# Routing of a mixture-of-experts layer built from unnormed rows, three token blocks ahead of the last

## What is computed

```python
x = x + jnp.concatenate([attn, ssm], axis=-1) @ w_out[i]
x = x + moe_ffn(rms_norm(x, norm_ffn[i]), w_router[i], b_router[i], ...)

def moe_ffn(h, w_router, b_router, w_gate, b_gate, w_up, b_up, w_down, b_down):
    t = h.reshape(-1, d)
    logits = (t @ w_router + b_router).astype(jnp.float32)
    top_val, top_idx = lax.top_k(logits, TOP_K)
    top_w = jax.nn.softmax(top_val, axis=-1)
    ...                      # the tokens of each expert are gathered
    g = jnp.minimum(xb @ w_gate[e] + b_gate[e], SWIGLU_LIMIT)
    u = jnp.clip(xb @ w_up[e] + b_up[e], -SWIGLU_LIMIT, SWIGLU_LIMIT)
    act = g * jax.nn.sigmoid(SWIGLU_ALPHA * g) * (u + 1.0)
    return act @ w_down[e] + b_down[e]   # weighted, scattered back, added
```

## Time and profile before

| | |
|---|---|
| median of 3 runs | 1453.48 us (1450.92 to 1461.56) |
| profiled execution | 1453.4 us, span 1451.6 us |
| mean granted TensorE clock | 0.954 |
| TensorE busy | 1320.3 us (91%) |
| VectorE, ScalarE, GpSimd busy | 443.3, 217.6, 192.5 us |
| moved by DMA | 446.16 MB, mean 307 GB/s |
| chain that ended last | TensorE 71%, SyncE's weight issues 19%, DMA 3% |

### The profile page before, as it was taken

How to read it: one execution, slowest core, us unless ns; L and a number is a source line. 1 busy time by engine, 2 the same in 40 slices (tenths; PEclk the granted TensorE clock), 3 DMA queues, 4 the chain that set the end, 5 groups by cost and what they waited for, 6 DMA issues and landing times.

```text
span 1451.6 us, 40133 instructions
## 1 busy us (share of the span) xinstructions
PE 1320.3 (91%) x18029; PEld 787.9 (54%) x18029; DVE 443.3 (31%) x1030; ACT 217.6 (15%) x491; POOL 192.5 (13%) x148
## 2 busy tenths in 40 slices
PE   5999989996799999899999999999999997876763
PEld 3466676664456656565666666666655554443321
DVE  3653576553322223122132312222222232112110
ACT  2222244341101110101010111111110110100000
POOL 0001300000102211211112121211111211111000
PEclk9999999997799999899999999999999999999765
DMA  8000420019899999999999999999999999999993
GB/s 344 3 1 0 163 88 1 30 49 347 310 352 376 382 391 401 391 393 360 389 387 392 381 381 391 363 385 383 386 386 388 392 380 398 398 395 393 402 406 136
DMA packets 128494, 446.16 MB, mean 307 GB/s; under 512 B 13218, under 2 KB 21474, under 8 KB 128322
## 3 DMA queue, kind: packets, MB, share of 16 engines
q1 hardware_dynamic: 113202, 426.37, 75.5%
q0 software_dynamic: 15120, 17.20, 5.6%
HBM read 433.29 MB, written 14.94 MB: 309 GB/s over the span
## 4 chain that ended last, share of the span: by engine, by line
PE 71%; SPq 19%; DMA 3%; DVE 2%; issue 2%; POOL 1%; ACT 1%; DVEq 0%; POOLq 0%; ACTq 0%
PE pair L1789 46%; SPq L596 18%; PE pair L1548 8%; PE pair L1532 4%; PE pair L1509 2%; PE pair L1640 2%; DMA ring<-in_w_down 1%; PE pair L1749 1%; PE pair L1729 1%; DMA ring<-in_w_in 1%; PE pair L1761 1%; PE pair L1652 1%; DVE rest L1032 1%; POOL ring L699 1%; DMA out<-rest 1%
## 5 line engine op out<-in xcount | busy, mean ns | idle before, releaser
L1789 PE MATMUL pair<-ring,rest 128*32 128x256 f32 x14864 | 864.0, 387 | 52.2 <-DMA ring<-in_w_down 20.1
L1789 PEld LDWEIGHTS pair<-ring,rest 128*32 128x32 f32 x14864 | 473.3, 111 | 391.4 <-issue 46.4
L1032 DVE TENSOR_TENSOR rest<-pair,rest 128x512 f32<-128x512 f32 (+5 forms) x122 | 90.6, 743 | 515.2 <-PE pair L1789 465.5
L751 POOL DMA_INDIRECT out<-rest x82 | 128.5, 1567 | 826.4 <-ACT rest L989 753.6
L1548 PE MATMUL pair<-ring 128*128 128x512 f32 (+1 forms) x320 | 125.3, 550 | 0.0
L989 ACT ACTIVATE rest<-rest 128x256 f32<-128x256 f32 x82 | 36.5, 500 | 568.1 <-DVE rest L1032 568.1
L1548 PEld LDWEIGHTS pair<-ring 128*128 128x128 f32 x320 | 60.3, 190 | 60.4 <-issue 58.8
L1032 DVE TENSOR_TENSOR rest<-rest 128x512 f32<-128x512 f32 (+7 forms) x98 | 62.4, 649 | 34.3 <-ACT rest L971 26.7
L971 ACT ACTIVATE rest<-rest 128x512 f32<-128x512 f32 (+3 forms) x34 | 24.4, 718 | 298.1 <-DVE rest L1341 298.1
L1789 PE MATMUL pair<-rest 128*32 128x256 f32 x880 | 55.7, 395 | 5.7 <-DMA rest<-in_w_gate 3.0
L1532 PE MATMUL pair<-ring 128*128 128x512 f32 x128 | 55.4, 594 | 0.0
(11 more groups left out here) (171 smaller groups left out, 807.0 us busy)
## 6 DMA issues: line engine op xcount, KB each, us to landing
ring<-in_w_up SPq DMA_DIRECT2D x121, 1024.0 KB, 17.3
ring<-in_w_gate SPq DMA_DIRECT2D x120, 1024.0 KB, 15.4
ring<-in_w_down SPq DMA_DIRECT2D x120, 1024.0 KB, 17.9
rest<-in_w_gate SPq DMA_DIRECT2D x8, 1024.0 KB, 17.4
rest<-in_w_down SPq DMA_DIRECT2D x8, 1024.0 KB, 15.9
rest<-in_w_up SPq DMA_DIRECT2D x7, 1024.0 KB, 16.1
ring<-in_w_in SPq DMA_DIRECT2D x1, 4160.0 KB, 15.5
ring<-in_x SPq DMA_DIRECT2D x8, 512.0 KB, 5.9
```

The source lines that it names most:

```text
L751: p.indirect_dma_start(out=out_rows, out_offset=bass.IndirectOffsetOnAxis(ap=sidx[vi.ring][:, g:g + 1].bitcast(I32), axis=0), in_=yrow[:, ...
L1032: return v.tensor_tensor(out=out, in0=a, in1=b, op=op)
L1789: last = T.matmul(ps[q * TOK:(q + 1) * TOK, g * QW:(g + 1) * QW], x, pieces[slot][:, kk, q * QW:(q + 1) * QW], start=(k == 0 and g % 2 == ...
```

## The change

- The router logits no longer wait for the norm. TensorE transposes the sum rows x1 themselves: half `th..a` inside the second half of the output projection (ahead of its last two k-slices), half `th..b` one step later; `th` and `lg` move one step forward. The gain `norm_ffn` is multiplied into the router matrix once by GpSimd (new; one more small DMA at the start brings it), and rstd is applied when the logits are read. `hrw` is still computed and stored as before.
- Choosing the top 4, weights and payload are done per tile on VectorE and ScalarE (`choose`, `weigh`; GpSimd's seven operations go). For tiles 0 to 2 they run while TensorE projects tile 3, with a new prefix product (`cue`, six matmuls) between the two halves of that projection.
- After the last logits only `cum` of tile 3, the last one-hot tile and the dispatch of expert 0 stand ahead of its gather. The order of the experts is computed behind it.
- `replicate` of expert 0, `dispatch` and `replicate` of expert 1 move from ahead of the products into the first gate product (ahead of k-slices 1, 2 and 3), the overflow table into the first up product. `dispatch` of expert j+2 moves from k-slice 4 to 5.
- Weight pieces 13 and 14 are issued after the `normed_rows` stores have landed, with 15 and 16.

```diff
-        for first, name, parts in ((TM, "tm", "ab"), (OP, "op", "ab"), (TH, "th", "ab"), (LG, "lg", " ")):
+        for first, names in ((TM, ("tm{}a", "tm{}b")), (OP, ("op{}a", "op{}b", "th{}a")), (TH, ("th{}b",)), (LG, ("lg{}",))):
...
-TM, OP, TH, LG = 7, 8, 10, 11
+TM, OP, TH, LG = 7, 8, 9, 10
...
             sp.wait_ge(s_ost, 16 * NT)
-            for n in (13, 14):
-                load(n, STREAM[n][1])
             sp.wait_ge(s_hst, 16 * NT)
             wait_full(sp, f"lg{NT - 1}")
-            for n in (15, 16):
+            for n in (13, 14, 15, 16):
                 load(n, STREAM[n][1])
...
+            nc.gpsimd.tensor_tensor(out=wr, in0=wr, in1=over(pc_ffn, NE), op=ALU.mult).then_inc(s_wrg, 1)
...
-            for k in range(TOPK):
-                link(p.tensor_tensor(out=oh[k], in0=oh[k], in1=over(ws[:, :, k], NE), op=ALU.mult))
-            link(p.tensor_tensor(out=wgt, in0=oh[0], in1=oh[1], op=ALU.add))
-            link(p.tensor_tensor(out=tmpp, in0=oh[2], in1=oh[3], op=ALU.add))
-            link(p.tensor_tensor(out=payload[:, :, :, 1], in0=wgt, in1=tmpp, op=ALU.add))
...
+                    copy_out(f"th{t}a", hrT[:, 0:4, :])
                     wait_taken(act, f"op{t}a")
                     wait_taken(act, f"op{t}b")
...
+            def choose(t):
+                link(v.tensor_copy(ixf[:, t, :], ix8[:, t, :].bitcast(U32)))
+                link(tt(chosen[:, t, :, :], times(iota[:, 0:NE], TOPK), over(ixf[:, t, 0:TOPK], NE), ALU.is_equal))
+                v.tensor_reduce(out=msk[:, t, :], in_=chosen[:, t, :, :].rearrange("p k e -> p e k"), axis=AX.X,
+                                op=ALU.add).then_inc(s_cnt, 1)
...
+                    if t == NT - 1:
+                        for c in range(t):
+                            choose(c)
+                        for c in range(t):
+                            weigh(c)
+                        ps = wait_full(dve, "cue")
+                        freed(place(posm[:, 0:t, :], ps[:, 0:t * NE], msk[:, 0:t, :]), "cue")
+                        wait_taken(dve, "cue")
+                        onehot_tiles(visit_at[0][0], 0, range(t))
...
+                    freed(v.tensor_copy(hrT[:, 4:8, :], cut(ps[:, :], 4, P)), f"th{t}b")
                     dve.wait_ge(s_x1n, t + 1)
...
-                    for h in range(2):
-                        project(f"op{t}{'ab'[h]}", t, h * 512, h * 512 + 512, hTm, w_out)
+                    project(f"op{t}a", t, 0, 512, hTm, w_out)
+                    if t == NT - 1:
+                        before_last_tile()
+                    ps = begin(f"op{t}b")
+                    for k in range(KT):
+                        if k == KT - 2:
+                            wait_taken(pe, f"op{t}a")
+                            transposes(f"th{t}a", [x1[:, t, n * P:(n + 1) * P] for n in range(4)])
+                        last = T.matmul(ps[:, :], hTm[:, k, t * P:(t + 1) * P], w_out[:, k, 512:DM],
+                                        start=(k == 0), stop=(k == KT - 1))
+                    end(last, f"op{t}b")
...
+                    else:
+                        during_gate[1] = lambda: replicate(v0)
+                        during_gate[2] = lambda: dispatch(v1)
+                        during_gate[3] = lambda: replicate(v1)
+                        during_up[1] = over_table
                     if j + 2 < NE:
-                        during_gate[4] = lambda: each(dispatch, visit_at[j + 2])
+                        during_gate[5] = lambda: each(dispatch, visit_at[j + 2])
```

More of the change, by code:

```diff
@@ L90 @@
 NV = len(VISITS)
+OVER_TABLE = ("o", None, 0)
 def turning_uses():
@@ L1285, in _ @@
[L1285 to L1294 removed]
+            choose(NT - 1)
@@ L1295, in onehots @@
+            weigh(NT - 1)
+            ps = wait_full(dve, "cum")
+            freed(place(posm[:, NT - 1:NT, :], ps[:, 0:NE], msk[:, NT - 1:NT, :]), "cum")
+            wait_taken(dve, "cum")
+            def onehots(vi, e, tiles=range(NT)):
+                if vi.n:
+                    if back := next((w for w in every_visit[vi.n - 1::-1] if (w.off > 0) == (vi.off > 0)), None):
                         wait_turned(dve, back.turns["d", 0])
-                buf = cut((onehot_x if vi.off else onehot)[:, 0:NT * c], NT, c)
@@ L1642, in attend, with before_last_tile @@
                 last.then_inc(s_of, 1)
+            def before_last_tile():
+                pe.wait_ge(s_cnt, NT - 1)
+                ps = begin("cue")
+                for t in range(NT - 1):
+                    for k in range(t + 1):
+                        last = T.matmul(ps[:, t * NE:(t + 1) * NE], ones if k < t else c_lt, msk[:, k, :],
+                                        start=(k == 0), stop=(k == t))
+                end(last, "cue")
             for t in range(NT):
@@ L1815, in _, with over_table @@
             for b in range(RINGB):
[L1816 removed]
+                turns = sum(1 for _, bb in where.values() if bb == b)
                 pe.wait_ge(psum_free[b], turns)
[L1818 to L1826 removed]
+            turn_rows(v0)
+            def over_table():
+                pe.wait_ge(s_ovf, 1)
+                use = at_turn[OVER_TABLE]
+                ps = turning(use)
+                turned(T.matmul(ps[:, 0:2 * IW], ones, rhs2.rearrange("p a b -> p (a b)"), start=True, stop=True), use)
             for j in range(NE + 1):
```

224 lines of the change are left out of this document (105 added, 119 removed).

## The result

The changed kernel took 1459.53 us, the median of 6 runs (1457.64 to 1461.68), against 1453.51 us (6 runs, 1450.92 to 1461.56). The ratio is 1.0037, with an interval of 1.0020 to 1.0053: 6.0 us slower, 0.4%, within the 1% that I had called no change. 1456 had been forecast, with a range of 1446 to 1464. The profiled execution took 1459.62 us, with a span of 1457.5 and a mean clock of 0.952 (before 1453.4, 1451.6 and 0.954).

What follows compares the result with a forecast made beforehand. The weight stream was taken to set the end, with TensorE pacing it by giving slots back. A restart 2.2 us later and a pace 3.8 later were taken as 3: 1453.4 + 3, say 1456 us, range 1446 to 1464.

Steps and rivals of the forecast that it cites:

- What bounds: Before the first product: last projection, six pieces, store, gather, transposes form the chain; an earlier start could win 7.1 us.
- the routing stands beside this chain: Ahead of expert 0's gather: routing ended 2.4 us before needed; indices moving from 363 to about 355 us are worth 0.
- What is added to the chain: Around the last projection: `cue` 1.45 us, four transposes 0.55, earlier shift 0.5; its reading and the store come 2.5 us later.
- The shift ahead of the projection: Before the last projection: half `th..a` in tile 2's projection and VectorE's work add 0.5 us, bounds 0 and 1.2.
- rival D: First products: small matmul groups keep the clock at 1.2 GHz, costing 16.7 us, 1473 us in all; chance 0.05.
- Gather and first product: From store to first product: gather takes 8.6 us, product starts at 378.7 us, 1.7 later; bounds 1.4 earlier, 2.4 later.
- Work put into the first products: Until expert 1's rows are transposed: `dispatch`, a second `replicate` and the overflow product add 2.1 us, at most 3.4.
- Held-back pieces 13 and 14: Weight stream before the first products: holding them back costs nothing, since nothing in the ring is needed until about 381 us.
- the pace term: Expert products: where TensorE paces the stream it is 3.8 us later; with loads restarting 2.2 later, 3 was taken.
- B: Last `normed_rows` store: overtakes the pieces, landing in 3 us; first product near 367 us, time 1446 us; chance 0.12.
- C: Weight stream from 384 us: ahead at all times, it swallows the delay; only the restart counts, 1453 us; chance 0.12.
- E: Expert 1's gather: issued about 6.8 us after the start, its rows come too late; TensorE stands 4 us, 1460; chance 0.04.

Runs made afterwards that it cites:

- Experiments 1 and 2: Last `normed_rows` store moved from SyncE's to ScalarE's queue, in the kernel before (1453.05 us) and in the changed kernel (1449.09 us).
- b_act: Kernel before with the last `normed_rows` store issued on ScalarE's queue instead of SyncE's: 1453.05 us, ratio 0.9992.
- a_fill: Changed kernel with two filler matmuls, ahead of the last tile's mixed-row transposes and ahead of its projection: 1457.09 us, ratio 1.0031.
- b_delay: Kernel before with eight filler matmuls between the halves of the last projection: 1463.46 us, ratio 1.0064.
- a_spfirst: Changed kernel with SyncE issuing the last `normed_rows` store ahead of weight pieces 7 to 12: 1449.93 us, ratio 0.9974.
- combo2: Changed kernel with the edits of a_act, a_hooks and a_cue, plus the two filler matmuls of a_fill: 1443.99 us, ratio 0.9929.
- a_act: Changed kernel with the last `normed_rows` store issued on ScalarE's queue instead of SyncE's: 1449.09 us, ratio 0.9956.
- a_hooks: Changed kernel with `replicate` of expert 0 and `dispatch` and `replicate` of expert 1 back ahead of the first product: 1459.29 us, ratio 1.0027.
- a_cue: Changed kernel with `cue` moved behind the last projection and its reading behind `hrw`: 1459.47 us, ratio 1.0035.
- combo1: Changed kernel with the edits of a_act, a_hooks and a_cue together: 1446.3 us, ratio 0.9943.

## Why the prediction was right, and which term was mis-sized

- **What bounds: right, by a narrow margin.** The chain last projection, six pieces, store, gather, transposes stands in the trace after as forecast: GpSimd released by the store, the store landing in 16.6 us, the indices written at 356.6 where 355 was estimated. Experiments 1 and 2 show both halves of "the routing stands beside this chain". In the kernel before that sentence holds for expert 0's indices and not for the whole routing: the overflow table held the transposes until 0.85 us after the gather had landed, as the prediction says, and the profile's own chain runs through the logits (348.78 us), the dispatch (361.37 us) and the table (373 to 374.85 us). That is why b_act gains nothing.
- **What is added to the chain: mechanism right, size wrong.** The step "Sum: the projection of the last tile is read 1.45 + 0.55 + 0.5 = 2.5 us later" measured 4.8. `cue` and `th..a` measured 1.3 and 0.4. The shift ahead of the projection measured 1.1, near the upper bound of 1.2 and within the scatter between executions. The missing 2.1 us are the first half at the lower clock, for which the sum had no term at all: it took that half over at its old length. In a_fill, where the clock holds, the half takes 7.11 us. I had looked for a clock effect only among the first products, rival D.
- **Gather and first product:** 1.7 forecast, at most 2.4, and 3.9 measured, which is the 2.3 us of the term above carried on; gather (8.3 us against 8.6) and the 0.85 us of the overflow table behave as said.
- **Work put into the first products:** from the first product to expert 1's transposes it took 17.7 us before and 19.4 after, 1.75 more where 2.1 was forecast.
- **Held-back pieces 13 and 14 cost nothing: right in sum, though not for the reason given.** They do open a hole, 0.59 x 4 = 2.4 us at 368 to 372 us, while the pieces wait for the store; the later hole shrinks from 5.3 us to 0.80 x 4 = 3.2.
- **From TensorE's delay to the end:** I averaged a restart of 2.2 and a pace of 3.8 to 3. Measured, the loads restart 3.8 us later (386.22 against 382.42 us, SyncE's first piece into a freed slot) and the pace term is 5.6; the end, 6.0 to 6.2 us, is nearer to the pace term than to an average. Delays add up as empty time and are passed on, and b_delay shows no swallowing.
- **The range held, the case's own ends did not.** The forecast's upper end was 1459.2 us, and 1459.53 was measured. The result lies in the range because 1464 allowed for the spread of the runs, not because the sum was close: it had half of the loss. Of the signs, the first product (378 to 379 us) and the store's issue (350.5 us) came 2 us late, at 380.89 and 352.80.
- **Rivals.** B did not occur: the store did not overtake. Its price, 1446, left out what the change adds ahead of the pieces: where the store was freed, the empty time behind 350 us fell to 0.7 us and the time to 1449.1; in a_spfirst the first product started at 366.7 us, B's 367, and the time was 1449.9. With `cue` and the hooks moved back and the clock held, in combo2, it fell to 1444. The Trainium skill (DMA: Bandwidth & Descriptors, Queues, rings and completion order) says that descriptors of one ring are consumed in order, and that each DMA engine takes turns between queue rows packet by packet. By that, a store on another row should be served beside the pieces and not behind them; 7.5 us against 16.6 agrees. C fell with b_delay. D was the wrong place: the clock was back at 1.00 by 388 us in spite of the small groups among the products. E: expert 1's gather went out 7.0 us after the first product (6.8 forecast), and its transposes show no wait.

Two causes stay open. Why the last projection starts late, and by how much beyond the scatter, was not tried apart (one late copy on VectorE, L1024, released it and is the candidate). And the worth of `cue`'s place and of the hooks, 1 to 2 us in the traces, isn't resolved in the times.

## What to carry to other kernels

When a stream of loads sets the end, add up the time in which it stands empty, with its places, and price an edit by what it does to that sum, not by how early some engine starts. When two chains run side by side to the same event, shortening the one that isn't last is worth nothing until the other is shortened too: name both ends before moving work. And ask of each new wait on a matmul engine not only what stands behind it, but whether the clock of the long products behind it survives it.

## What the runs showed of the hardware that was not expected

- **The clock fell among short waits.** After the change, TensorE stood idle for 0.18, 0.51 and 0.83 us between small groups from 325.6 to 330.1 us, and was granted 0.50 from 327.2 to 334.0 us. It fell during the second of these waits, so the third, the longest, did not bring it down; in a_act and a_hooks it fell in the third, at about 331 us. In one trace of each kernel, the clock fell at the last tile in all six with the new order and no fillers (after, a_act, a_hooks, a_cue, a_spfirst, combo1). It did not in the three with the order of before, where TensorE waits once, for 2.17 us up to 325.37 us, nor in the four with two groups of fillers, 1.10 and 1.02 us long. That filling the gaps holds the clock is shown; which of the gaps or small groups lets it fall is not. The Trainium skill (TensorE: Matmul & The Clock Gate, A second HAM failure mode: psum-queue depth-cycling) tells, of another kernel, of small idles between groups of matmuls, frequent enough to let the clock swing. These rows agree that idles far shorter than the low stretch can go with a fall; here it was one fall and one rise, not a swing.
- **A 512 KB store has three prices.** 3.0 us with nothing queued ahead on its queue, 7.5 to 7.7 on ScalarE's queue beside six pieces on SyncE's, 16.5 to 17.3 behind the six on one queue. The Trainium skill (DMA: Bandwidth & Descriptors, Issuing engines are not separate DMA queues) says that issuing from several engines only saves sequencer time. For a small transfer behind large ones this does not hold here: it landed 9 us sooner.
